# Two blocks on one core: where the constants are fetched, and where one modulation product per layer stands

## Time and profile before

| | |
|---|---|
| median of 3 runs | 3120.54 us (3120.41, 3120.54, 3131.64) |
| the profiled execution | 3129.2 us, span 3127.4 us |
| PE, PEld, DVE, ACT, POOL busy | 95%, 81%, 52%, 41%, 5% of the span |
| granted TensorE clock, mean | 0.975 |
| weights and other input read | 439.65 MB, 141 GB/s over the span |

### The profile page before, as it was taken

How to read it: one execution, slowest core, us unless ns; L and a number is a source line. 1 busy time by engine, 2 the same in 40 slices (tenths; PEclk the granted TensorE clock), 3 DMA queues, 4 the chain that set the end, 5 groups by cost and what they waited for, 6 DMA issues and landing times.

```text
span 3127.4 us, 51125 instructions
## 1 busy us (share of the span) xinstructions
PE 2965.4 (95%) x17586; PEld 2533.1 (81%) x17586; DVE 1637.2 (52%) x3043; ACT 1291.8 (41%) x2519; POOL 167.0 (5%) x121
## 2 busy tenths in 40 slices
PE   7999899999998999999999878999999999989998
PEld 7978789799797897788886545788878888768998
DVE  5565765555647656533335796433335333448554
ACT  4444445455544455432332444323324323335553
POOL 0000010000010100000000670000000000000000
PEclk9999899999998999999999988999999999989999
DMA  7555265555652656533333762333314233241553
GB/s 256 184 163 199 72 202 178 174 183 182 181 161 69 220 179 177 172 108 95 104 97 114 256 223 81 121 95 96 105 54 139 92 106 98 81 143 50 175 181 98
DMA packets 239052, 443.10 MB, mean 142 GB/s; under 512 B 26400, under 2 KB 27424, under 8 KB 238240
## 3 DMA queue, kind: packets, MB, share of 16 engines
q1 hardware_dynamic: 237344, 432.94, 44.1%
q0 software_dynamic: 1536, 7.86, 0.8%
HBM read 439.65 MB, written 1.05 MB: 141 GB/s over the span
## 4 chain that ended last, share of the span: by engine, by line
PE 82%; DVE 12%; issue 2%; POOL 2%; ACT 1%; DMA 1%; SPq 0%; DVEq 0%; POOLq 0%; ACTq 0%
PE ps L736 81%; DVE low L1720 1%; DVE hidden L1723 1%; POOL hidden L2306 1%; DVE zl L1723 1%; DMA raw<-weights 1%; DVE ps L1723 1%; DVE hidden L1720 1%; DVE zl L1720 1%; DVE coef L2228 1%; DVE hidden L2232 1%; POOL low L2276 1%; DVE gated L1720 1%; DVE hidden L2055 0%; DVE neg_max L2028 0%
## 5 line engine op out<-in xcount | busy, mean ns | idle before, releaser
L736 PE MATMUL ps<-zh,low 128*128 128x256 f32 (+1 forms) x4192 | 1400.6, 334 | 79.1 <-DVE low L1720 41.1
L736 PE MATMUL ps<-zl,high 128*128 128x256 f32 (+1 forms) x4192 | 1381.8, 330 | 0.0
L736 PE MATMUL ps<-zh,high 128*128 128x256 f32 (+1 forms) x4192 | 1380.9, 329 | 0.0
L1720 DVE TENSOR_TENSOR low<-raw,high 128x512 fp32r<-128x512 f32 x1276 | 843.8, 699 | 462.1 <-ACT high L1277 460.3
L1277 ACT ACTIVATE high<-raw 128x512 fp32r<-128x512 f32 x1304 | 761.7, 625 | 572.6 <-PE ps L736 499.5
L736 PEld LDWEIGHTS ps<-zh,low 128*128 128x128 f32 x4192 | 806.0, 192 | 184.0 <-DVE low L1720 42.2
L736 PEld LDWEIGHTS ps<-zl,high 128*128 128x128 f32 x4192 | 806.7, 192 | 71.8 <-issue 4.8
L736 PEld LDWEIGHTS ps<-zh,high 128*128 128x128 f32 x4192 | 806.5, 192 | 69.1
L1720 DVE TENSOR_TENSOR hidden<-gated,ps 128x256 f32 (+1 forms) x176 | 91.5, 520 | 604.2 <-ACT gated L1277 604.2
L1277 ACT ACTIVATE gated<-ps 128x256 f32<-128x256 f32 (+1 forms) x176 | 81.3, 462 | 497.3 <-PE ps L736 497.1
L736 PE MATMUL ps<-high,zl 128*128 128x512 f32 (+2 forms) x544 | 195.2, 359 | 3.8 <-DVE zl L1720 3.8
(11 more groups left out here) (190 smaller groups left out, 2016.8 us busy)
## 6 DMA issues: line engine op xcount, KB each, us to landing
raw<-weights SPq DMA_DIRECT2D x1640, 256.0 KB, 3.4
hidden<-norms POOLq DMA_DIRECT2D x4, 1024.0 KB, 7.0
cst<-consts SPq DMA_DIRECT2D x1, 1829.0 KB, 14.3
x<-x_in SPq DMA_DIRECT2D x1, 1024.0 KB, 7.0
x<-tokens_in POOLq DMA_DIRECT2D x1, 1024.0 KB, 13.8
x<-ctx_in POOLq DMA_DIRECT2D x1, 1024.0 KB, 6.4
out<-hidden POOLq DMA_DIRECT2D x1, 1024.0 KB, 5.1
ple_p<-p_in POOLq DMA_DIRECT2D x1, 512.0 KB, 7.2
```

What stands on the lines that cost most here:

```text
L736: return nc.tensor.matmul(out, lhsT, rhs, start=first, stop=last, **kw)
L1720: return nc.vector.tensor_tensor(out, a, b, op)
```

## The change

Three things. SP brings the constants behind weight quarters 0 to 7 instead of behind quarter 1. The fill of the post norm after the mixer (`eps == 1`) is gone on all three engines, with its take of rows and columns. In its place stands a fill in the mixer, between the compressed scores and the transposes of their softmax, with bank 3 for its rows and bank 4 for the columns; the stream of weights has its 8 quarters ahead of `w_out` rather than behind it. `jobs` has a new `fills_out` ahead of the first transposes, which write bank 3. The number of fills, of bytes and of products is as before.

```diff
@@ stream
         yield ("phi2", l, 0, 2, True)
         yield fills.pop()
+        yield fills.pop()
         yield from (("rows", ("w_out", l), t, 2, False) for t in range(KT - 2))
         yield ("rows", ("w_out", l), KT - 2, 4, False)
-        yield fills.pop()
         yield from ffn(("ffn2", l))
@@ SP
             sp.dma_start(x[:, :, 0:S], x_in).then_inc(x_landed, 16)
-            load(0, weights[0])
-            load(1, weights[1])
-            sp.dma_start(cst[:], consts).then_inc(consts_landed, 16)
-            for n in range(2, RING):
+            for n in range(RING):
                 load(n, weights[n])
+                if n == 7:
+                    sp.dma_start(cst[:], consts).then_inc(consts_landed, 16)
@@ PE.post_norm (and Act.post_norm)
-                self.fill(2, 3)
+                if eps == 0:
+                    self.fill(2, 3)
@@ PE.mixer
                 m.then_inc(cmp_scores, 1)
+                self.fill(3, 4)
                 pe.wait_ge(cmp_probs, seen(cmp_probs))
@@ PE.jobs
                 for j in range(n + 3):
+                    if j == 2:
+                        self.fills_out()
@@ Dve.post_norm
-                pending = self.taken < self.fills
-                self.filled()
+                pending = eps == 0 and self.taken < self.fills
+                if eps == 0:
+                    self.filled()
```

## The result

The changed kernel takes 3138.89 us (median of 10 runs, 3130.83 to 3143.17) against 3124.1 for the kernel before in the same comparison (10 runs, 3119.51 to 3131.64). The ratio is 1.0036, with an interval of 1.0025 to 1.0048: 11 us slower, 8 to 15. That is outside the range predicted, on its slow side. The profiled execution has a span of 3141.3 us at a mean granted clock of 0.967 (before 3127.4 and 0.975).

A forecast was written before the change was run, and what follows sets the result against it. PE was taken as the bound, carrying 82% of the chain of waits. The terms -4.0 + 2 x 5.8 - 0.9 = +6.7 us on 3120.5 gave 3127 us, with a range of 3114 to 3132.

The forecast's parts named there:

- Part 1: Kernel start: constants behind quarter 7 let quarters 2 to 7 arrive sooner, -4.0 us, bounds -2 and -5.1.
- the rival in which the start gives nothing: Kernel start: PE catches up with quarters 8 to 11 and stands as long as before, +10.7 us, 3131; chance 0.10.
- Part 2a: Mixer's middle: turn of rows and fill at the low clock make PE's own chain 3.0 us late, beside the refill's wait.
- Part 2b: Mixer's middle: splits wait for three `w_out` quarters late in the ring's refill, +5.8 us per layer (4.6 to 7.2).
- Part 2c: Mixer's middle: the fill could bring the clock back, up to -4.0 us per layer; taken as 0 because PE then stands.
- The bound of -4.0 us: Jobs 0 to 3: most that could be gained per layer if the clock came back and stayed.
- The rival in which the stall is paid back by the clock: Mixer's middle: eighth quarter lands after 7.3 us and the clock stays up, -3.7 us in all, 3117; chance 0.22.
- Part 2d: Norm after the mixer without its fill: DVE loses a copy and an addition, -0.9 us for both layers (0 to -1.5).
- The sum: Whole kernel: -4.0 + 2 x 5.8 - 0.9 = +6.7 us.
- the four cases: Whole kernel: forecast 0.56, faster by the clock 0.22, slower by the norm's clock 0.12, no gain at the start 0.10.
- the 0.03 on either side of the range: Whole kernel: chance given to a change beyond 15.6 us from 3120.5, slower or faster, 0.03 each.
- The norm's clock as a rival: Norm after the mixer: PE loses the clock and splits do not cover it, +2 us per layer, 3131; chance 0.12.

The follow-up runs named there:

- the run with late splits: The changed kernel with the three splits of `w_out` moved from before the softmax to behind the compressed jobs: 3126.54 us, ratio 1.0011.
- the fill alone: The changed kernel with the order of the first transfers put back as it was before: 3139.44 us, ratio 1.0053.
- early-turn kernel: The changed kernel with `w_out` splits behind the jobs, look-ahead shorter by four, and PE turning the middle fill's rows some 6 us sooner: 3114.08 us, ratio 0.9954.

## Why the prediction was wrong, step by step

**Part 1, the start: right.** -4.0 was predicted, the first gate moved by -3.7 (over all twelve profiles it stands at 30.59 to 31.57 with the old start and at 26.15 to 27.43 with the new, 4.1 between the means), and the holds went as described. ACT waited 3.77 us for the constants behind quarter 7, yet PE stood for nothing there: low part 8 was there near 24.4 and PE's 96 matmuls ran until near 27.5, some 3 us of room where the prediction saw little. So the rival in which the start gives nothing at the start itself is out. What the sum didn't have is the dip of the clock further on.

**Part 2a, PE's own chain: right.** 3.0 us late at the low clock; with the splits gone, 2.8 in layer 0, and 1.0 where the turn was taken out of it.

**Part 2b, the refill: right mechanism, slightly small.** 5.8 us per layer were predicted from one high and one low part behind a landing at 328.3; measured 6.3 and 6.7. The 8.5 us from the first issue to the eighth quarter came true. The mis-sized piece is the issue: it was set 1.1 us after the start of the fill and came 1.95 after it (317.94 to 319.89), when its first four products were through. ACT's 4.05 us on DMA and DVE's 8.90 us behind it are the wait, and the run with late splits took it away. Both layers together: 13.0 in place of 11.6.

**Part 2c, the clock in the middle: right, with its reason.** 0.50 until 340, as the hole of 3.65 us stands behind the fill. In layer 0 of the fill alone the clock even came back behind the fill, and fell again while PE stood 5.35 us for the heads (granted clock 0.93, then 0.50):

```profile
323.00:327.00 4.00, 2.39 (x19) 1.72 (x18) 0.00 (x0) 0.87 (x2) 0.00 (x0) 0.93 0.97 333
327.00:332.00 5.00, 0.79 (x8) 0.82 (x9) 3.38 (x7) 2.33 (x6) 0.00 (x0) 0.50 0.20 77
```

The bound of -4.0 us was real: where the hole was closed, the clock came back for good in one of the two layers, and the jobs there lost 3 us or more. The rival in which the stall is paid back by the clock needed a landing quicker than the ring could give; it came true only in kernels without the wait.

**Part 2d, the norm: here the prediction failed, twice.** The step was: "The ring now holds 11 quarters of the feed-forward part; ACT did not wait for DMA there before, so nothing." I looked at the transfers of those quarters and not at their splits. The change makes eight quarters that nobody split into eight that ACT and DVE must split, in a place where the look-ahead reaches past the product's end, so they wait for PE and stand in front of the residual addition: +3.3 us per layer. What would have shown it is in the code, not in the trace: with four quarters of the output product left, `ahead(4)` reaches twelve on, eight past its end, and the stream's order says whether those are raw. The same eight splits are then missing from the norm. That makes it 3.6 and 3.8 us shorter up to the last `zl` (the copy and the addition included), of which PE's low clock takes 1.5 back: -2.1 and -2.3 us, not the -0.9 for both from a copy and an addition. Net of the step: +2.2 instead of -0.9.

**The sum** was therefore off by 0.3 + 1.4 + 3.1 = 4.8 us: 11.5 and not 6.7. The rest of the miss in the absolute figure is the base. It was set on 3120.54, the median of three runs; ten runs gave 3124.1, and ten of the changed kernel a median 14.8 above that, where the interval of the ratio has 8 to 15. The range, 3114 to 3132, held no case in which a term was missing; its bounds covered only the sizes of the terms that it had. The chances of the four cases add up to 1.00, so the 0.03 on either side of the range had no room beside them.

**The norm's clock as a rival: it came, hidden under a larger gain.** The prediction put the loss of the clock at nothing, because in layer 0 of the kernel before a fall had cost nothing. Those rows were of a norm with eight splits in it, where DVE's work was the bound. With the splits gone PE is never idle from its first transpose to the first gate, and the low clock costs 1.5 us in either layer, 3 in all, where the rival had 2 per layer. What brings it is PE's stand of 5.53 us, 3.3 of it from the late residual addition: with the addition on time PE stands 2.25 us, and the clock stays up or falls for 3.4 us in place of 6.8. The rule of the Trainium skill (TensorE: Matmul & The Clock Gate, Part 4: PE-mode transpose) on which that rival drew is that transposes don't count as busy for the clock in the same way; no run here tells whether that is so, since the clock was already low when they began, behind PE's stand.

## What to carry to other kernels

When a piece of raw work is moved in a shared ring of weights, look at both ends of the move: at the old place other quarters stand now, and whoever reads ahead there may have to work on them where he used to skip. Follow every `ahead` and every "make the low parts up to here" whose reach crosses the place, and ask what stands in the queue behind it. Ask of every stretch from which work is taken what bounds it next: a fall of the clock that cost nothing under DVE's splits cost 1.5 us when they were gone. A fill put into a latency-bound chain can pay through the clock: here it did so in one of two layers once no long hole was left behind it, and in none with the hole; and a base time from one profile should be checked for dips of the clock with a second before small terms are summed against it.

## What the runs showed of the hardware

I had not expected that one kernel meets a fall of the granted clock in one profile and not in the next, at the same place in the work and with the same price each time: 3.1 us behind the start of the first mixer (1.4 to 1.5 when it lasts half as long), 1.6 us in its output product, and the first of them while PE was busy without a break (10.00 of 10 us, clock 0.82). Stages without such a dip repeat from profile to profile within 0.4 us in most rows of the table. Terms below 3 us can therefore be read from stage durations, and not from one kernel's total against another's. Nor had I expected that a float32 fill of 16 instructions could stand at the end of the slow stretch in the mixer's middle: in layer 0 of the early-turn kernel the windows have 0.50, then 0.88 where it ends, then 1.00, and in layer 1 of the same profile, with the same instructions, it stayed at 0.50 (the fill took 3.64 us again). What decides between the two is open.
